# Mixer of a hybrid SSD/GLA layer: the router's product with its columns as the weights, in four column groups, added up one step later

## The chip, the cores and the metric

One core of one Trainium2 chip runs the whole program (one layer: modulation, input projection, two scans, mixer, mixture of experts, final norm). The metric is the device time of one execution in microseconds; lower is better. Below, T, L, P, N stand for names of the kernel; times are written in us.

## The reference, cut to what matters

The change lies in the stage that computes the token mixers' output, the residual, the second norm and the router's logits, for 2048 tokens in 16 tiles of 128 (D_MODEL = 1024, 32 experts):

```
mix = concat([y, o], -1) @ w_out
x = x + m_lat[2] * mix
h2 = modulate(rmsnorm(x, norm2_g), m_lat[3], m_lat[4])
s = jax.nn.sigmoid((h2 @ w_router).astype(jnp.float32))     # 2048 x 32
```

The product `h2 @ w_router` is what the change computes in another way. The scale of the modulation is applied to the tokens before it, and its shift enters as one row that is added to the logits (`rt_shift`).

## The kernel before, in words

`mixer` is written by hand, engine by engine; each engine runs its own list in the order of the code, and the engines meet only in semaphores. Its main loop has 18 steps n = 0 to 17 over 16 tiles (LT = 16). In a step three tiles are in work: `now` = n, `before` = n - 1 and `done` = n - 2 (`tiles(n)`).

TensorE's order in a step: `attn(now)` (L1626, eight products into `at`), `ssd(now)` (L1603 and L1611, into `py`), `turned_m(before)` (L1562, eight transposes into `tr`), `gla(now)` (L1644 and L1649, into `po`), `turned_x(done)` (L1570, eight transposes into `at`), `project(before)` (L1581, 48 products of 512 columns into `tr`) and `router(done)` (L1592). The router's product takes eight slices of 128 features: the turned tokens `xsT` (128x128) are the weights, the router's 32 columns `w_rt` the moving data, and the 128x32 result builds up in `po[:, 0, 256:288]`. Each f32 product stands in the trace as two passes.

VectorE's order: `masked_attn(now)` (L1768 twice, L1773), `state_mid` and `state_next` (L1688 to L1704), `split_m(before)` (L1755), `gated_y` (L1780, L1784), `segment` (L1732, L1738), `gated_o` (L1805, L1808), `decayed_scores` and `decayed_c` (L1746, L1751), then `residual(before)` (L1790), `scaled_x(before)` (L1798) and `logits(done)` (L1760). ScalarE ends a step with `squares_x(before)` (L1505), whose sum GpSimd turns into a reciprocal root (L1438, L1441) for `scaled_x`. `gla(now)` waits for both `both_done` (L1773) and `mid_done` (L1688) of the same step:

```
            def gla(t):
                r, qd = rec[t % 2], qks[t % 2][:, 0, :, :]
                pe.wait_ge(both_done, t + 1)
                pe.wait_ge(mid_done, t + CT + 1)
```

Elsewhere in the program two products already stand in the form with column groups: `slab_products` (L264) and the small columns of the input projection (L664), each `pe.matmul(acc[32 * j:32 * j + 32, ...], ...)` with j = k % 4.

The stage ends with a barrier of all engines (L1296 is the line of the semaphores' and the block's end); the next stage, `slots`, reads the logits.

Of the kernel before, what the change touches and what calls it, by code (L numbers as in the profile page):

```python
# [17 lines left out]
ALU = mybir.AluOpType  # L18
ACT = mybir.ActivationFunctionType
F32 = mybir.dt.float32  # L20
I32 = mybir.dt.int32
AX = mybir.AxisListType.X

P = 128
D = 1024
KT = D // P
# [6 lines left out]
LT = SEQ // P  # L33
SH, SP_, SN = 8, 64, 64
SW = SH * SP_
# [14 lines left out]
NE, NG, EG = 32, 8, 4  # L50
# [1239 lines left out]
def mixer(nc, A, C, K, route, tok_rec, feat_rec, back_state, fwd_chunk, qk_rec, a_rows, zg_rec, w_gated, x_mid, h_rows):  # L1290
    mod, ident = C["mod"], C["ident"]
# [4 lines left out]
    with ExitStack() as ctx:  # L1296
        sem = Names(nc, ctx, "mix")

        def sb(name, shape, dt=F32):
            return ctx.enter_context(nc.sbuf_tensor(f"{name}_m", shape, dt))  # L1300

        def ps(name):
            return ctx.enter_context(nc.psum_tensor(f"{name}_m", [P, 2, 512], F32))

        rec = [K["rec"][b][:, T_X:T_GF] for b in (2, 1)]
# [3 lines left out]
        st = [sb(f"st{b}", [P, 3, 256]) for b in range(2)]  # L1309
        abc = sb("abc", [P, 2, SH, P])  # L1310
        cs = sb("cs", [P, 2, 4, P])
        w_hi, w_lo = sb("w_hi", [P, KT, D], F32R), sb("w_lo", [P, KT, D], F32R)
        w_rt, rt_shift = sb("w_rt", [P, KT, NE]), sb("rt_shift", [P, NE])
        scale_bc, skip = sb("scale_bc", [P, D]), sb("skip", [P, SH])
        E, other = sb("E", [P, SH, P]), sb("other", [P, 4, P])
        M = sb("M", [P, SH, P])
# [5 lines left out]
        xs, xsT = sb("xs", [P, D]), sb("xsT", [P, KT, P])  # L1322
        ssm, ssx = sb("ssm", [P, 8]), sb("ssx", [P, 1])
        rs, rsx = sb("rs", [P, 8]), sb("rsx", [P, 1])
        py, po, at, tr = ps("py"), ps("po"), ps("at"), ps("tr")
# [18 lines left out]
        mt_ps, hi_done, lo_done, op_ps = (sem(n) for n in ("m_transposed", "m_hi_done", "m_lo_done", "out_product"))  # L1344
        x_added, x_sq, x_rs, xs_done, rows_added = (
            sem(n) for n in ("x_added", "x_square", "x_rstd", "x_scaled", "rows_added"))
        xt_ps, xt_done, log_ps, log_done = (sem(n) for n in ("x_transposed", "xT_done", "logits_product", "logits_done"))
        block = ctx.enter_context(nc.Block())

        def tiles(n):  # L1350
# [114 lines left out]
        @block.scalar  # L1465
        def _(act):
            def split_m(t, n):
                act.wait_ge(mt_ps, 2 * t + n + 1)
                act.activation(m_hi[:, 4 * n:4 * n + 4, :], tr[:, n, :].rearrange("p (a b) -> p a b", a=4), ACT.Copy).then_inc(hi_done, 1)

            def decays(t, g):
                act.wait_ge(seg_done, 2 * t + g + 1)
                act.activation(E[:, 4 * g:4 * g + 4, :], E[:, 4 * g:4 * g + 4, :], ACT.Exp).then_inc(seg_exp, 1)

            def inter_decays(t):
                act.wait_ge(cs_loaded, 64 * t + 64)
                act.activation(cs[:, :, :, :], cs[:, :, :, :], ACT.Exp).then_inc(cs_exp, 1)

            def turned_x(t):
                if t:  # L1480
                    act.wait_ge(log_ps, t)
                for n in range(2):
                    act.wait_ge(xt_ps, 2 * t + n + 1)
                    act.activation(xsT[:, 4 * n:4 * n + 4, :], at[:, n, :].rearrange("p (a b) -> p a b", a=4), ACT.Copy).then_inc(xt_done, 1)

            def squares_y(t):
                act.wait_ge(y_gated, t + 1)
                if t:
                    act.wait_ge(y_rs, t)
                    act.wait_ge(o_sq, 4 * t)  # L1490
                if t >= 2:
                    act.wait_ge(x_sq, t - 1)
                act.activation(junk[:, 0:SW], m[:, 0:SW], ACT.Square, scale=SW ** -0.5, accum_out=ssm[:, 4:5]).then_inc(y_sq, 1)

            def normed_y(t):
                act.wait_ge(y_rs, t + 1)
                act.activation(m[:, 0:SW], m[:, 0:SW], ACT.Copy, scale=rs[:, 4:5]).then_inc(y_done, 1)

            def squares_x(t):
                act.wait_ge(x_added, 2 * t + 2)  # L1500
                if t:
                    act.wait_ge(x_rs, t)
                act.wait_ge(y_sq, min(t + 2, LT))
                act.wait_ge(o_sq, 4 * min(t + 2, LT))
                act.activation(junk[:, :], x1[t % 2][:, :], ACT.Square, scale=D ** -0.5, accum_out=ssx[:, :]).then_inc(x_sq, 1)  # L1505

            def squares_o(t):
                act.wait_ge(o_ps, t + 1)
                if t:
                    act.wait_ge(o_rs, t)  # L1510
                act.wait_ge(y_sq, t + 1)
                for h in range(GH):
                    act.activation(junk[:, GV * h:GV * (h + 1)], po[:, h % 2, P * (h // 2):P * (h // 2 + 1)], ACT.Square, scale=GV ** -0.5,
                                   accum_out=ssm[:, h:h + 1]).then_inc(o_sq, 1)

            decays(0, 0)
            decays(0, 1)
            inter_decays(0)
            for n in range(LT + 2):
                now, before, done = tiles(n)  # L1520
                if before is not None:
                    split_m(before, 0)
                    split_m(before, 1)
                if now is not None:
                    squares_y(now)
                    squares_o(now)
                    normed_y(now)
                if done is not None:
                    turned_x(done)
                if now is not None:  # L1530
                    if now + 1 < LT:
                        decays(now + 1, 0)
                        decays(now + 1, 1)
                        inter_decays(now + 1)
                if before is not None:
                    squares_x(before)
                    act.dma_start(x_mid_t[before], x1[before % 2][:, :]).then_inc(x1_stored[before % 2], 16)

        @block.tensor
        def _(pe):  # L1540
# [45 lines left out]
            def router(t):  # L1586
                pe.wait_ge(xt_done, 2 * t + 2)
                pe.wait_ge(o_normed, min(t + 3, LT))
                if t:
                    pe.wait_ge(log_done, t)  # L1590
                for k in range(KT):
                    mm = pe.matmul(po[:, 0, 256:256 + NE], xsT[:, k, :], w_rt[:, k, :], start=(k == 0), stop=(k == KT - 1))  # L1592
                mm.then_inc(log_ps, 1)

            def ssd(t):
                h_f, h_b = st[t % 2], bst[t % 2]
# [58 lines left out]
            for n in range(LT + 2):  # L1655
                now, before, done = tiles(n)
                if now is not None:
                    attn(now)
                    ssd(now)
                if before is not None:  # L1660
                    turned_m(before, 0)
                    turned_m(before, 1)
                if now is not None:
                    gla(now)
                if n == 0:
                    router_shift()
                if done is not None:
                    turned_x(done)
                if before is not None:
                    project(before, range(KT))  # L1670
                if done is not None:
                    router(done)

        @block.vector
        def _(dve):
# [16 lines left out]
            def state_next(i, t):  # L1692
# [10 lines left out]
                dve.wait_ge(decayed, i + 1)  # L1703
                dve.tensor_tensor(nxt[:, 0, :], nxt[:, 0, :], f[:, 0:256], ALU.add).then_inc(next_done, 1)  # L1704

            for n, spread in enumerate((scale_bc, shift_bc)):
                dve.wait_ge(spread_ps, n + 1)
                for h in range(2):
                    dve.tensor_copy(spread[:, 512 * h:512 * h + 512], tr[:, h, :]).then_inc(spread_done, 1)
# [47 lines left out]

            def logits(t):
                dve.wait_ge(log_ps, t + 1)
                dve.tensor_tensor(route["logits"][:, t, :], po[:, 0, 256:256 + NE], rt_shift[:, :], ALU.add).then_inc(log_done, 1)  # L1760

            def masked_attn(t):
                if t:
# [50 lines left out]
            for n in range(LT + 2):  # L1814
                now, before, done = tiles(n)
                more = now is not None and now + 1 < LT
                if now is not None:
                    masked_attn(now)
                    state_mid(now + CT, now)
                    state_next(now + CT, now)  # L1820
                if before is not None:
                    split_m(before, 0)
                    split_m(before, 1)
                if now is not None:
                    gated_y(now)
                if more:
                    segment(now + 1, 0)
                    segment(now + 1, 1)
                if now is not None:
                    gated_o(now)  # L1830
                if n == 0:
                    router_shift()
                if more:
                    decayed_scores(now + 1)
                    decayed_c(now + 1)
                if before is not None:
                    residual(before)
                    scaled_x(before)
                if done is not None:
                    logits(done)  # L1840


TAB = MAXB + 4
# [635 lines left out]
```

## Time and profile before

| | us |
|---|---|
| median of 3 runs | 2337.08 (2336.34 to 2339.93) |
| the profiled execution's own time | 2337.34 |
| its span in the trace | 2335.5 |
| TensorE busy over the span | 2134.6 (91%) |
| VectorE busy | 1663.0 (71%) |
| ScalarE busy | 1159.2 (50%) |
| the mixer stage, from its first to its last work | about 855.6 to 1262 |

A row of the trace gives start, duration, engine, line and operation, output <- inputs; PE is TensorE's product, PEld its weight load, DVE VectorE, ACT ScalarE, POOL GpSimd. A duration of a product runs to the modelled arrival of its result, so rows of one engine overlap; how fast products follow on each other is read from starts.

### The profile page before, as it was taken

What the parts mean: (1) busy time and instruction counts of PE and PEld (TensorE: products, weight loads), DVE (VectorE), ACT (ScalarE), POOL (GpSimd) and SP (SyncE); (2) the same over time, 40 slices, a digit from 0 to 9 for tenths busy, and PEclk for the clock granted to TensorE, in tenths of its full rate; (3) what the DMA queues carried; (4) which work ended last, traced back from release to release, by engine and by line L of the source; (5) the groups of instructions that cost most, each with busy time, mean ns of one, the idle gap of its engine ahead of it and who ended that gap; (6) DMA issues with size and microseconds to landing.
All of it is one profiled execution on the core that took longest, in us unless ns stands there. A gap on an engine that the chain in (4) does not pass through costs nothing. (4 is left out here: it accounts for less than half of the span.)

```text
span 2335.5 us, 36752 instructions
## 1 busy us (share of the span) xinstructions
PE 2134.6 (91%) x11905; PEld 1734.7 (74%) x11905; DVE 1663.0 (71%) x2123; ACT 1159.2 (50%) x1499; POOL 513.7 (22%) x535
## 2 busy tenths in 40 slices
PE   5999999998999979999994499999999999999980
PEld 3888888886778768888883478778787878878760
DVE  2444444445776777677764789999999999999983
ACT  1233333334555533333331177777777777777763
POOL 1000000000010122233221123333332333343332
PEclk8999999998999997999996699999999999999995
DMA  8233333333888859898865345578978689899957
GB/s 329 68 120 120 120 120 120 120 111 104 307 300 301 309 176 362 290 309 289 306 186 165 142 141 174 162 235 277 334 237 289 209 258 369 265 328 312 373 167 300
DMA packets 209166, 537.27 MB, mean 230 GB/s; under 512 B 14896, under 2 KB 45611, under 8 KB 202539
## 3 DMA queue, kind: packets, MB, share of 16 engines
q1 hardware_dynamic: 176056, 424.71, 50.7%
q0 software_dynamic: 30512, 102.77, 16.9%
q10 hardware_dynamic: 2499, 8.45, 0.9%
q8 instruction: 63, 1.03, 0.2%
q14 instruction: 36, 0.29, 0.0%
HBM read 402.28 MB, written 133.61 MB: 229 GB/s over the span
## 5 line engine op out<-in xcount | busy, mean ns | idle before, releaser
L2217 ACT ACTIVATE w_hi_e<-w_gates 128x2048 fp32r (+1 forms) x103 | 197.9, 1923 | 212.1 <-issue 103.4
L2343 DVE TENSOR_TENSOR w_lo_e<-w_gates,w_hi_e 128x2048 fp32r<-128x2048 f32 x103 | 236.2, 2294 | 34.1 <-ACT w_hi_e L2217 34.1
L2343 DVE TENSOR_TENSOR w_lo_e<-w_ups,w_hi_e 128x2048 fp32r<-128x2048 f32 x102 | 233.3, 2288 | 36.9 <-ACT w_hi_e L2217 36.9
L2343 DVE TENSOR_TENSOR w_lo_e<-w_downs,w_hi_e 128x2048 fp32r<-128x2048 f32 x100 | 228.4, 2284 | 0.0
L2217 ACT ACTIVATE w_hi_e<-w_ups 128x2048 fp32r (+1 forms) x102 | 195.7, 1918 | 24.9 <-PE pd_e L2290 22.5
L2217 ACT ACTIVATE w_hi_e<-w_downs 128x2048 fp32r x100 | 191.6, 1916 | 0.8
L650 PE MATMUL pf<-raws,w_in_sb 128*128 128x256 f32 x800 | 176.1, 382 | 1.1 <-DVE raws L726 1.1
L2290 PE MATMUL pg_e<-w_hi_e,x_hi_e 128*128 128x512 f32 x408 | 167.7, 411 | 7.3 <-DVE w_lo_e L2343 7.3
L650 PEld LDWEIGHTS pf<-raws,w_in_sb 128*128 128x128 f32 x800 | 152.8, 192 | 22.5 <-DVE raws L726 1.5
L2195 POOL DMA_INDIRECT x_mid<-yb_e,to_e x50 | 127.6, 2551 | 185.1 <-DVE yb_e L2387 183.1
L2290 PE MATMUL pd_e<-w_hi_e,h_hi_e 128*128 128x512 f32 x400 | 162.2, 405 | 0.0
L2290 PE MATMUL pg_e<-w_lo_e,x_hi_e 128*128 128x512 f32 x408 | 161.9, 397 | 0.0
L2290 PE MATMUL pg_e<-w_hi_e,x_lo_e 128*128 128x512 f32 x408 | 161.8, 397 | 0.0
L2290 PE MATMUL pd_e<-w_hi_e,h_lo_e 128*128 128x512 f32 x400 | 157.9, 395 | 0.0
L2290 PE MATMUL pu_e<-w_hi_e,x_hi_e 128*128 128x512 f32 x400 | 157.8, 395 | 0.0
L2290 PE MATMUL pu_e<-w_hi_e,x_lo_e 128*128 128x512 f32 x400 | 157.8, 395 | 0.0
L2290 PE MATMUL pu_e<-w_lo_e,x_hi_e 128*128 128x512 f32 x400 | 157.8, 395 | 0.0
L2290 PE MATMUL pd_e<-w_lo_e,h_hi_e 128*128 128x512 f32 x400 | 157.8, 395 | 0.0
L2174 POOL COPY idx_e<-toks 128x1 int32 (+1 forms) x54 | 50.5, 936 | 450.3 <-DMA x_mid<-yb_e,to_e 341.9
L650 PE MATMUL pf<-hT,w_in_sb 128*128 128x256 f32 x640 | 139.5, 379 | 0.0
L650 PEld LDWEIGHTS pf<-hT,w_in_sb 128*128 128x128 f32 x640 | 121.3, 190 | 16.5
L757 DVE TENSOR_SCALAR fm<-u_raw,cols 128x256 f32<-128x256 f32 x54 | 18.3, 408 | 146.8 <-ACT u_raw L536 146.8
(423 smaller groups left out, 4839.2 us busy)
## 6 DMA issues: line engine op xcount, KB each, us to landing
w_gates<-in_w_gate_dram SPq DMA_DIRECT2D x32, 2048.0 KB, 11.9
w_ups<-in_w_up_dram SPq DMA_DIRECT2D x32, 2048.0 KB
w_downs<-in_w_down_dram SPq DMA_DIRECT2D x32, 2048.0 KB
w_mod_half<-in_w_mod_dram SPq DMA_DIRECT2D x16, 1024.0 KB, 6.6
abc_m<-a_rows SPq DMA_DIRECT2D x16, 1024.0 KB, 4.9
recs<-tok_rec SPq DMA_DIRECT2D x15, 968.0 KB, 7.8
qk_rec<-qk SPq DMA_DIRECT2D x14, 1024.0 KB, 3.9
qk<-qk_rec SPq DMA_DIRECT2D x14, 1024.0 KB
```

The costliest lines, as they stand in the source:

```text
L650: mm = pe.matmul(pf[n % 2][:, f, :], w[:, k, c0:c0 + P], h[:, k, :], start=(k == 0), stop=(k == KT - 1))
L757: i = dve.tensor_scalar(a, b, wt, cols[:, R_CB + f:R_CB + f + 1], ALU.mult, ALU.add)
L2174: pool.tensor_copy(idx[u][:, :], toks[:, bass.ds(b, 1), 0]).then_inc(idx_ready, 1)
L2195: pool.indirect_dma_start(out=x_mid, out_offset=bass.IndirectOffsetOnAxis(ap=to[u][:, 0:1], axis=0), in_=yb[:, :], in_offset=None, compute ...
L2217: act.activation(w_hi[:, s % 3:s % 3 + 1, :], raw(part, half, place), ACT.Copy).then_inc(hi_done, 1)
L2290: mm = pe.matmul(acc[:, :], a[:, k, :], w[:, s % 3, c], start=start and n == 0, stop=stop and n == 2)
L2343: dve.tensor_tensor(w_lo[:, s % 3:s % 3 + 1, :], raw(part, half, place), w_hi[:, s % 3:s % 3 + 1, :].bitcast(F32), ALU.subtract).then_inc( ...
```

## The change

The router's columns become the weights: for slice k the 32 columns `w_rt[:, k, :]` are loaded into column group j = k % 4 of the array, and the tokens `xsT[:, k, :]` (128 columns) stream past. Slices 0 to 3 start, slices 4 to 7 add, so four partial sums of 32x128 build up on partitions 32j to 32j + 31 of `po[:, 0, 256:384]`. ScalarE copies them into `quarters` (a part of a buffer of the stage before), and a product of `quarters` with `sum4` (128x32: four identities, one under another) adds the four and turns the result back to 128x32. This small product stands in the next step between `attn` and `ssd`; the logits' addition on VectorE moves from the end of a step to behind `masked_attn` of the next.

```diff
+        sum4, quarters = K["st"][0][:, 0, 0:NE], K["rec"][0][:, D + SW:D + SW + P]
...
             def turned_x(t):
                 if t:
-                    act.wait_ge(log_ps, t)
+                    act.wait_ge(quarter_ps, t)
...
+            def quartered(t):
+                act.wait_ge(quarter_ps, t + 1)
+                if t:
+                    act.wait_ge(log_ps, t)
+                act.activation(quarters[:, :], po[:, 0, 256:256 + P], ACT.Copy).then_inc(quarter_done, 1)
...
                         inter_decays(now + 1)
+                if done is not None:
+                    quartered(done)
                 if before is not None:
                     squares_x(before)
...
                 for k in range(KT):
-                    mm = pe.matmul(po[:, 0, 256:256 + NE], xsT[:, k, :], w_rt[:, k, :], start=(k == 0), stop=(k == KT - 1))
-                mm.then_inc(log_ps, 1)
+                    j = k % 4
+                    mm = pe.matmul(po[32 * j:32 * j + 32, 0, 256:256 + P], w_rt[:, k, :], xsT[:, k, :], start=(k < 4), stop=(k >= 4))
+                mm.then_inc(quarter_ps, 1)
+
+            def logit_sums(t):
+                pe.wait_ge(quarter_done, t + 1)
+                pe.wait_ge(sum4_done, 1)
+                pe.matmul(po[:, 0, 256 + P:256 + P + NE], quarters[:, :], sum4[:, :], start=True, stop=True).then_inc(log_ps, 1)
...
                     attn(now)
+                if n >= 3:
+                    logit_sums(n - 3)
+                if now is not None:
                     ssd(now)
...
+            logit_sums(LT - 1)
...
+            dve.tensor_reduce(sum4[:, :], ident[:, :].rearrange("p (j c) -> p c j", j=4), AX, ALU.add).then_inc(sum4_done, 1)
...
                     masked_attn(now)
+                if n >= 3:
+                    logits(n - 3)
+                if now is not None:
                     state_mid(now + CT, now)
...
-                if done is not None:
-                    logits(done)
+            logits(LT - 1)
```

What this moves on the engines is shown at one step boundary. TensorE, from the end of `project` of one step to `turned_m` of the next; the names are output <- weights or moving data, and the line numbers differ between the two kernels. Before:

```order
L1581 MATMUL tr_m<-w_hi_m,m_lo_m 128x512 x2
L1592 MATMUL po_m<-w_rt_m,xsT_m 128x32 x8
L1626 MATMUL at_m<-qk 128x128 x8
L1603 MATMUL py_m<-recs,M_m 128x64 x8
L1611 MATMUL py_m<-st_m,cs_m 128x64 x8
```

Now (`st` and `recs` in the fourth row are `sum4` and `quarters`):

```order
L1592 MATMUL tr_m<-w_hi_m,m_lo_m 128x512 x2
L1604 MATMUL po_m<-xsT_m,w_rt_m 32x128 x8
L1643 MATMUL at_m<-qk 128x128 x8
L1610 MATMUL po_m<-st,recs 128x32
L1620 MATMUL py_m<-recs,M_m 128x64 x8
L1628 MATMUL py_m<-st_m,cs_m 128x64 x8
```

The eight products keep their place, with their operands exchanged, and one product has come in ahead of `ssd`. VectorE over the same boundary, before:

```order
L1790 TENSOR_TENSOR x_m<-tr_m,x_m 128x512 x2
L1798 SCALAR_TENSOR_TENSOR xs_m<-x_m,rsx_m,scale_bc_m 128x1024
L1760 TENSOR_TENSOR logits<-po_m,rt_shift_m 128x32
L1768 TENSOR_TENSOR am_m<-at_m,incl_bd 128x512 x2
L1773 TENSOR_TENSOR both_m<-am_m 128x512
```

Now:

```order
L1812 TENSOR_TENSOR x_m<-tr_m,x_m 128x512 x2
L1820 SCALAR_TENSOR_TENSOR xs_m<-x_m,rsx_m,scale_bc_m 128x1024
L1790 TENSOR_TENSOR am_m<-at_m,incl_bd 128x512 x2
L1795 TENSOR_TENSOR both_m<-am_m 128x512
L1782 TENSOR_TENSOR logits<-po_m,rt_shift_m 128x32
L1709 SCALAR_TENSOR_TENSOR st_m<-st_m,fc 128x128 x2
```

The logits' addition has moved past three instructions and stands ahead of `state_mid` still. ScalarE at the end of a step, now (`recs<-po_m` is the copy of the quarters; the row was not there before, the others were):

```order
L1480 ACTIVATE cs_m<-cs_m 128x1024
L1493 ACTIVATE recs<-po_m 128x128
L1514 ACTIVATE recs,ssx_m<-x_m 128x1024
L1548 DMA x_mid<-x_m 128x1024
```

The copy has come in between the exponentials and `squares_x`.

## Rows read from the trace of the kernel before

**Rows 1.** The page: busy time of each engine over the span.
```profile
PE 2134.6 (91%) x11905; PEld 1734.7 (74%) x11905; DVE 1663.0 (71%) x2123; ACT 1159.2 (50%) x1499; POOL 513.7 (22%) x535
```

**Rows 2.** Stretches: one step; PE, PEld, DVE, ACT, POOL busy, clock, DMA, GB/s.
```profile
1093.36:1115.63 22.27, 22.27 (x186) 19.15 (x185) 16.33 (x28) 7.79 (x20) 6.92 (x9) 1.00 0.91 302
```

**Rows 3.** Timeline, TensorE, steps 9 to 10: start, us, engine, line, operation.
```profile
1093.36 1.98 PEld L1592 LDWEIGHTS po_m<-w_rt_m,xsT_m 128*128 128x128 f32 x16
1093.59 1.87 PE L1592 MATMUL po_m<-w_rt_m,xsT_m 128*128 128x32 f32 x16
...
1095.38 1.16 PE L1626 MATMUL at_m<-qk 64*128 64x128 f32 x16
...
1100.34 0.86 PEld L1562 LDWEIGHTS tr_m<-ident,m_m 128*128 128x128 f32 x8
...
1101.24 0.52 PEld L1644 LDWEIGHTS po_m<-recs,both_m 128*128 128x128 f32 x4
...
1103.13 0.45 PE L1649 MATMUL po_m<-st_m,qk 64*64 64x128 f32 x8
...
1103.72 0.86 PEld L1570 LDWEIGHTS at_m<-ident,xs_m 128*128 128x128 f32 x8 [0.17 <-issue]
...
1104.55 0.30 PEld L1581 LDWEIGHTS tr_m<-w_hi_m,m_hi_m 128*128 128x128 f32 x2
```

**Rows 4.** The same timeline: VectorE, ScalarE and GpSimd; in brackets idle time and releaser.
```profile
1093.63 1.29 DVE L1790 TENSOR_TENSOR x_m<-tr_m,x_m 128x512 f32<-128x512 f32 x2 [2.33 <-PE tr_m L1581]
1094.95 1.06 ACT L1505 ACTIVATE recs<-x_m 128x1024 f32<-128x1024 f32 x1 [6.25 <-DVE x_m L1790]
...
1096.57 0.57 POOL L1441 TENSOR_TENSOR rsx_m<-rsx_m,mhalf_m 128x1 f32<-128x1 f32 x1
1097.27 1.28 DVE L1798 SCALAR_TENSOR_TENSOR xs_m<-x_m,rsx_m,scale_bc_m 128x1024 f32<-128x1024 f32 x1 [2.35 <-POOL rsx_m L1441]
...
1098.47 0.18 DVE L1760 TENSOR_TENSOR logits<-po_m,rt_shift_m 128x32 f32<-128x32 f32 x1
1098.57 1.28 DVE L1768 TENSOR_TENSOR am_m<-at_m,incl_bd 128x512 f32<-128x512 f32 x2
...
1100.57 0.61 DVE L1688 SCALAR_TENSOR_TENSOR st_m<-st_m,fc 128x128 f32<-128x128 f32 x2
```

**Rows 5.** Timeline of step 2, the step without a router's product ahead of it.
```profile
921.64 0.68 PE L1644 MATMUL po_m<-recs,both_m 128*128 128x128 f32 x4 [1.77 <-DVE both_m L1773]
...
926.45 0.72 PE L1581 MATMUL tr_m<-w_hi_m,m_hi_m 128*128 128x512 f32 x2
```

**Rows 6.** Stretches behind that wait, and the stage's start; columns as in rows 2.
```profile
922.50:925.70 3.20, 3.20 (x37) 2.32 (x30) 3.17 (x6) 0.41 (x1) 0.00 (x0) 0.50 1.04 207
926.00:945.00 19.00, 19.00 (x140) 16.51 (x139) 11.59 (x19) 6.09 (x17) 6.92 (x9) 1.00 0.84 312
855.60:864.20 8.60, 4.07 (x32) 3.69 (x32) 5.69 (x12) 1.24 (x1) 0.06 (x1) 1.00 0.90 281
```

**Rows 7.** Timeline of the input projection: column groups with 256 moving columns.
```profile
203.12 0.56 PEld L664 LDWEIGHTS psm<-raws,w_small 128*32 128x32 f32 x12 [0.30 <-issue]
203.12 1.05 PE L664 MATMUL psm<-raws,w_small 128*32 128x256 f32 x16
204.10 0.50 PE L630 MATMUL pz<-wv_hi,x_hi 128*128 128x512 f32 x1
```

**Rows 8.** Timeline, ScalarE: one square of 128x128 read from `po`.
```profile
1105.76 0.28 ACT L1513 ACTIVATE recs<-po_m 128x128 f32<-128x128 f32 x1
```

**Rows 9.** Timeline, VectorE, the stage's first work; a reduction of 128 elements.
```profile
857.73 1.29 DVE L1709 COPY scale_bc_m<-tr_m 128x512 f32<-128x512 f32 x2 [0.44 <-PE tr_m L1545]
1269.03 0.29 DVE L1983 TENSOR_REDUCE best_r<-gscore_r 128x16 f32<-128x128 f32 x1
```

**Rows 10.** The stage's end: timeline, and line L1296 (ns min/median/max, starts).
```profile
1253.81 3.62 PE L1592 MATMUL po_m<-w_rt_m,xsT_m 128*128 128x32 f32 x16 [0.69 <-ACT xsT_m L1484]
1257.46 0.19 DVE L1760 TENSOR_TENSOR logits<-po_m,rt_shift_m 128x32 f32<-128x32 f32 x1 [6.27 <-PE po_m L1592]
...
L1296 POOLq DRAIN  x1: 3972/3972/3972, 1257.3 to 1257.3; - x1
L1296 SPq EVENT_SEMAPHORE  x1: 17/17/17, 1261.4 to 1261.4; - x1
```

More of the change, by code:

```diff
@@ L1346, in mixer @@
             sem(n) for n in ("x_added", "x_square", "x_rstd", "x_scaled", "rows_added"))
-        xt_ps, xt_done, log_ps, log_done = (sem(n) for n in ("x_transposed", "xT_done", "logits_product", "logits_done"))
+        xt_ps, xt_done, quarter_ps, quarter_done, log_ps, log_done = (
+            sem(n) for n in ("x_transposed", "xT_done", "logit_quarters", "quarters_copied", "logits_product", "logits_done"))
+        sum4_done = sem("sum_4_done")
         block = ctx.enter_context(nc.Block())
@@ L1759, in logits @@
                 dve.wait_ge(log_ps, t + 1)
-                dve.tensor_tensor(route["logits"][:, t, :], po[:, 0, 256:256 + NE], rt_shift[:, :], ALU.add).then_inc(log_done, 1)
+                dve.tensor_tensor(route["logits"][:, t, :], po[:, 0, 256 + P:256 + P + NE], rt_shift[:, :], ALU.add).then_inc(log_done, 1)
             def masked_attn(t):
```

## The prediction, before the change was run

> **What bounds the kernel now.** I read the page first, then stretches of the mixer, then its timeline, engine by engine. The page makes TensorE the suspect: 91% of the span [rows 1]. The stretch of one whole step of the mixer's loop says it more strongly: TensorE is busy for 22.27 of 22.27 us at the full clock, VectorE for 16.33, ScalarE for 7.79 [rows 2]. By that view alone, whatever shortens a product shortens the step. The timeline shows what it hides. Call T the start of the router's first weight load, which stands right behind the last projection product: 1093.36 [rows 3]. From T two chains run side by side until `gla`.
>
> TensorE's: router (to 1095.38), `attn`, `ssd`, then eight transposes whose first load starts at 1100.34, then `gla`, whose first load starts at 1101.24, that is T + 7.88 [rows 3].
>
> The other: the last projection product lets VectorE add the residual (1093.63, 1.29), ScalarE square (1094.95), GpSimd take the root (1096.57), VectorE scale (1097.27), add the logits (1098.47), mask the attention scores (1098.57), add them and update the state; `state_mid` starts at 1100.57 and runs 0.61, so ends at 1101.18 = T + 7.82 [rows 4]. VectorE's 2.33 and 2.35 of idle time in this chain are latency, not slack.
>
> `gla` waits for both. Its load starts 0.06 after `state_mid` ends. Would it have started earlier without that wait? The same eight transposes stand a second time in a step, where nothing is waited for behind them: load 1103.72 to the next load 1104.55, 0.83 [rows 3]. From 1100.34 that gives 1101.17, where `gla` loads at 1101.24. So TensorE arrives 0.07 before the state is there: the two chains end together, and VectorE's is the later one by a hair. The 100% busy step is the sum of two halves, of which one (T to `gla`) is set by the chain over four engines.
>
> **The change, part by part**, as times after T.
>
> *Router's product.* Before: T to the first `attn` product, 2.02 (16 passes of a full 128x128 load, 1.79 / 16 = 0.11 each) [rows 3]. Now 16 passes, four at a time, of 128 moving columns. The trace has no such row; two are near. `gla`'s own 16 passes of 128 f32 columns on four tiles of 64x64, which start at 1103.13 with the transposes following at 1103.72: 0.59 with the change of tile size behind it [rows 3]. And the input projection's 16 passes on the very 128x32 tiles, but with 256 columns: 203.12 to 204.10, 0.98 [rows 7]. I take 0.59, since the columns agree, and keep 0.98 as the upper end. Ahead of it stand 0.23 in which the last projection product streams (1093.36 to 1093.59) and, an estimate from how much of the 0.59 is not passes, 0.1 for the change of tile size. So `attn` starts at about T + 0.92 (at most 1.31), 1.1 earlier (at least 0.7).
>
> Here the Trainium skill speaks against the change: TensorE: Matmul & The Clock Gate, Part 3, says that weight loads overlap running products only when their row groups differ, and four column groups share all rows. By that rule the loads would line up with the products (the second rival prices this). The trace disagrees: twelve loads of L664 lie in 0.56 from 203.12 on, inside the products' time [rows 7].
>
> *The small product.* Two passes with a full load and 32 columns, 2 x 0.11 = 0.22, on TensorE between `attn` and `ssd`. It waits for ScalarE's copy, see next; TensorE gets there at about T + 2.1, so it doesn't wait.
>
> *ScalarE's copy.* The last pass's result is there at about T + 1.0 (at most 1.4). The copy reads 128x128 from `po`, as the squares of `gla`'s result do in 0.28 [rows 8]; with 0.05 for the semaphore it ends at T + 1.33 (at most 1.73). Queued behind it is `squares_x`, a link of the chain that sets the step; it needs ScalarE at 1094.95 = T + 1.59 [rows 4]. So the copy fits by 0.26; at the upper end it is late by 0.14, in each of 15 steps (n = 2 to 16): +2.1. I take 0. ScalarE is idle for 6.25 before that point [rows 4], which covers it.
>
> *The logits' addition.* It leaves the place ahead of `masked_attn`, where it costs 0.10 (1098.47 to 1098.57) [rows 4], and returns behind it, still ahead of `state_mid`. `both` comes 0.10 earlier, `state_mid` does not: T + 7.82 as before. I take 0; if the short addition were hidden at its new place, 13 x 0.10 = -1.3 would follow.
>
> *What comes of it on TensorE.* It reaches `gla` 1.1 - 0.22 = 0.88 earlier, T + 6.9, and waits there for the state until T + 7.88. From `gla`'s load to the end of `project` nothing is changed (3.31 to 1104.55, then 48 products). **Steps 3 to 15 (13 of them) gain 0.** In step 16 there is no `gla`; `turned_x` waits for `scaled_x`, which is the same chain: 0. `ssd` ends earlier, so the DMAs that wait for it are issued some 0.9 earlier for data wanted most of a step later: 0.
>
> *The start.* The reduction that makes `sum4` is new on VectorE, about 0.29 (a reduction of 128 elements), and stands where VectorE waits 0.44 for TensorE [rows 9]: 0. Without that cover it would cost 0.3 once.
>
> *The end.* In step 17 the last router's product runs at the reduced clock, 3.62, and the last logits end at 1257.65 [rows 10]. With groups, copy and small product this ends about 1 us earlier. But the stage ends for GpSimd: its queue drains for 3.97 from 1257.3 (behind the last store's landing), and all engines go on at 1261.4 [rows 10]. The cover is 3.6 us, so: 0.
>
> **The sum** is 0 against the profiled execution's 2337.34, which lies 0.26 above the median of the runs, 2337.08. Forecast 2337.0.
>
> **The rivals.**
>
> *1. TensorE is the bound after all* (busy all 22.27 [rows 2]). Then each of 13 steps gives 0.88: -11.4, about 2326. Against it: `gla`'s load starts 0.06 to 0.07 after `state_mid`'s end in each of these steps alike, and step 2, which has no router's product ahead of it, shows the outcome already: TensorE waits 1.77 ahead of `gla` for VectorE [rows 5]. Chance 0.04.
>
> *2. The copy comes late and holds up `squares_x`.* It decides from the point where the copy ends after T + 1.59, so where the product's result comes after T + 1.26. If the passes kept their old 0.11: 0.33 + 1.79 + 0.28 = T + 2.4, the copy ends at 2.73, 1.14 late, 15 times: +17, about 2354. Against it: the two rows of four tiles. Over 0.2% needs 0.31 per step, twice what my upper end leaves. Chance 0.02. If on top of that loads and products took turns, 0.11 and 0.11 per pass, it would be 16 x 0.11 = 1.8 more in each step, 15 x 2.9 = +44, about 2381: chance 0.01, since the loads there do overlap [rows 7]. (That is what the Trainium skill's rule on row groups, named above, would come to here.)
>
> *3. The clock.* The wait that takes the place of the work is about 0.95 in each of 13 steps. In step 2, behind TensorE's wait of 1.77, the granted clock stood at 0.50 from 922.5 to 925.7, and at 1.00 again from 926 [rows 5, 6]; from `gla` to `project` it took 926.45 - 921.64 = 4.81, where a step at full clock takes 3.31: a price of 1.5. Every step hit: 13 x 1.5 = +19.5, about 2356.5; it goes past 0.2% (4.7) with four steps of 13. For it: the section from T to `gla` is already thin work. Against it: the wait is about half as long, and at the stage's start TensorE was busy for 4.07 of 8.60 us with the clock at 1.00 throughout [rows 6]. Chance 0.06 for four steps or more, and about 0.1 for one to three (+1.5 to +4.5).
>
> **How the numbers follow.** A measurement of this kernel tells about 0.2%, 4.7 us, from no change. My own case, no change of the path, has 0.87 with the small clock cases in it; its time is 2337.0. The range reaches down by the 1.3 of the hidden addition and 1 for the spread of runs, to 2334.7, and up by the 2.1 of the copy, or two steps hit by the clock (3.0), and the same 1: 2341.0. Faster by over 0.2%: rival 1 and what I have not thought of, 0.05. Slower by over 0.2%: rivals 2 and 3, 0.09. Within: 0.86.
>
> **What would show it.** Right: the new product's rows from its first product to `attn` near 0.6; the copy ending before 1.59 after T; a new idle time of TensorE ahead of `gla`, about 0.9, put down to VectorE, in 13 steps; steps of 22.27 as before; the clock at 1.00 from 926 to the last steps. TensorE's busy time falls by some 10 us while the span stays. Wrong: steps shorter than 22.2 (the chain was not the bound); `squares_x` later than 1.59 after T (rival 2); stretches at 0.50 between 930 and 1230, and steps of about 23.8 (rival 3).

## The result, and the profile after

| | before | after |
|---|---|---|
| median of 16 runs each, same chip | 2338.32 (2333.64 to 2343.31) | 2342.12 (2337.90 to 2347.41) |
| ratio, 95% interval | | 1.0016 (1.0009 to 1.0022) |
| profiled execution, its span | 2337.34, 2335.5 | 2342.06, 2340.3 |

The median lies 1.1 us above the upper end of the range, 2341.0. The ratio stays under the 0.2% that was called a difference, but its interval excludes 1: the change costs a little, where the forecast was nothing. By the ratio alone the change costs 2.1 to 5.1 us. Of the 5.1 us between the forecast of 2337.0 and the median, 1.3 are not the change's: the forecast took the median of three runs, 2337.08, and the same kernel's median over 16 runs, those three among them, is 2338.32. It was 2338.53 to 2338.84 in the three later comparisons with many runs too.

The page's busy line of the changed kernel, to [rows 1], and one row of its costliest groups (engine, tile, count; busy and mean ns; idle time ahead of it, most of it without a releaser, "issue"):

```profile
PE 2120.3 (91%) x11937; PEld 1712.7 (73%) x11937; DVE 1663.1 (71%) x2124; ACT 1163.0 (50%) x1515; POOL 509.9 (22%) x535
...
L2241 ACT ACTIVATE w_hi_e<-w_gates 128x2048 fp32r (+1 forms) x103 | 197.9, 1923 | 213.8 <-issue 107.8
```

TensorE is busy for 14.3 us less (2134.6 before) and the span is no shorter. One step of the loop, columns as in [rows 2], a stretch of the whole loop, and the stretch behind the wait in step 2, which answers to the first of [rows 6]:

```profile
1094.94:1117.21 22.27, 21.52 (x188) 17.80 (x186) 16.33 (x28) 8.06 (x21) 6.92 (x9) 1.00 0.91 313
...
930.00:1230.00 300.00, 289.85 (x2476) 239.26 (x2474) 211.12 (x362) 104.51 (x274) 88.55 (x118) 1.00 0.83 274
...
921.50:928.00 6.50, 6.17 (x49) 5.09 (x50) 6.43 (x14) 2.02 (x11) 1.46 (x3) 0.50 1.06 299
```

The timeline of that step answers to [rows 3, 4]. T is 1094.94 here, counted back from the residual's addition, which starts 0.27 behind T in both kernels:

```profile
1095.21 1.29 DVE L1812 TENSOR_TENSOR x_m<-tr_m,x_m 128x512 f32<-128x512 f32 x2 [2.35 <-PE tr_m L1592]
1095.26 0.64 PE L1604 MATMUL po_m<-xsT_m,w_rt_m 128*32 128x128 f32 x16
1095.84 1.16 PE L1643 MATMUL at_m<-qk 64*128 64x128 f32 x16
1095.97 0.28 ACT L1493 ACTIVATE recs<-po_m 128x128 f32<-128x128 f32 x1 [5.71 <-PE po_m L1604]
1096.54 1.06 ACT L1514 ACTIVATE recs<-x_m 128x1024 f32<-128x1024 f32 x1 [0.28 <-DVE x_m L1812]
1096.93 0.41 PE L1610 MATMUL po_m<-st,recs 128*128 128x32 f32 x2
...
1102.15 0.60 DVE L1709 SCALAR_TENSOR_TENSOR st_m<-st_m,fc 128x128 f32<-128x128 f32 x2
1102.83 0.52 PEld L1661 LDWEIGHTS po_m<-recs,both_m 128*128 128x128 f32 x4 [0.96 <-DVE both_m L1795]
1102.86 0.68 PE L1661 MATMUL po_m<-recs,both_m 128*128 128x128 f32 x4 [0.75 <-DVE st_m L1709]
```

The reader is to see three things. The sixteen passes take 0.58 (1095.26 to 1095.84). The copy (L1493) is over at 1096.25, 0.29 before `squares_x` (L1514). And `gla` now has a wait ahead of it, 0.96 on its weight load, put down to VectorE. The load starts at 1102.83, 0.08 after `state_mid` ends (1102.15 + 0.60 = 1102.75). `gla` starts at T + 7.89, where it started before at T + 7.88: the work taken from TensorE became that wait.

**Where the profiled execution's +4.8 of span lies**, from marks that both timelines have (starts of the same products in each):

| stretch | before | after | |
|---|---|---|---|
| start of the program to T of step 1 | 913.50 | 913.45 | -0.05 |
| T of step 1 to T of step 2 | 24.00 | 25.62 | +1.62 |
| step 3 | 22.26 | 22.26 | 0 |
| steps 4 to 15 | 267.20 | 267.21 | +0.01 |
| step 16 | 18.94 | 19.18 | +0.24 |
| from there to the first work of `slots` | 16.40 | 18.19 | +1.79 |
| to the sixth block of the experts' loop | 160.84 | 160.74 | -0.10 |
| experts' loop from there to its last product, 23 rounds | 842.04 | 843.03 | +0.99 |
| the rest | 70.34 | 70.61 | +0.27 |

The mixer's thirteen steps hold none of it. Three places hold nearly all of it, and the forecast named none of them as a cost. The first is step 2, which has no router's product ahead of it: after its wait the granted clock stood at 0.50 (1.2 GHz, the lower of its two levels; 1.00 is 2.4 GHz) for 3.4 us before [rows 6] and for 6.8 us now. The second is the stage's end: the last store of `h_rows` landed 7.4 after its issue where it took 5.7 before, and GpSimd's drain, 3.97 as in [rows 10], began at 1260.9 instead of 1257.3:

```profile
L1296 POOLq DRAIN  x1: 3972/3972/3972, 1260.9 to 1260.9; - x1
```

The third is the experts' loop, whose code the change does not touch. The runs had to say which of these the change causes and which differ from one execution to the next anyway.

### The profile page after: what moved, and what is told of

Same layout as the page of the kernel before. It is cut to its first block and busy times, and to the rows that moved or that the text cites. A ratio compares the mean times of both kernels' runs of the same rounds, so it can differ in the third digit from the quotient of the medians.

```text
span 2340.3 us, 36863 instructions
## 1 busy us (share of the span) xinstructions
PE 2120.3 (91%) x11937; PEld 1712.7 (73%) x11937; DVE 1663.1 (71%) x2124; ACT 1163.0 (50%) x1515; POOL 509.9 (22%) x535
## 3 DMA queue, kind: packets, MB, share of 16 engines
q8 instruction: 63, 1.03, 0.2%
## 5 line engine op out<-in xcount | busy, mean ns | idle before, releaser
L2241 ACT ACTIVATE w_hi_e<-w_gates 128x2048 fp32r (+1 forms) x103 | 197.9, 1923 | 213.8 <-issue 107.8
## 6 DMA issues: line engine op xcount, KB each, us to landing
w_ups<-in_w_up_dram SPq DMA_DIRECT2D x32, 2048.0 KB, 16.3
```

The source lines that it names most:

```text
L2241: act.activation(w_hi[:, s % 3:s % 3 + 1, :], raw(part, half, place), ACT.Copy).then_inc(hi_done, 1)
```

## The experiments

Theory A: the wait that replaced TensorE's work costs clock (rival 3 in another dress). Theory B: the first result is scatter of executions. Theory C: the last store of the mixer lands later with the change, and the stage's end with it. Theory D: the changed kernel gives ScalarE 31 instructions more (16 copies, 15 semaphore waits) ahead of the experts' loop, and where the loop lies in its program sets the time of the loop's edge.

**Both kernels again.** The kernel before, unchanged.

> The kernel before, a second time, for a second profile of it and for the noise of the comparison. All theories: ratio 1.000 with an interval of about 0.1%. Theory A (the clock): behind TensorE's wait in step 2 and in step 16 the granted clock falls to 0.50 here as well, for a time that differs from execution to execution, 3 to 7 us; the 13 steps in between are 22.27 each. Theory C (the last store): the last store of the mixer lands 5.7 us after its issue, as in the first profile of this kernel (7.5 in that of the changed one); theory B (scatter) says that it differs between executions of one kernel, so it may be 7 here.

Measured: 2336.89, ratio 0.9994 (0.9985 to 1.0003). The same program against itself came out 0.6 thousandths off, so less than about 1.5 us is nothing that a single comparison shows.

> The changed kernel, a second time. Theory A: slower than before by about 4 us (1.0016), with more time at clock 0.50 than the kernel before has, in step 16 above all, where TensorE now idles about 1 us longer. Theory B: the 3.8 us are mostly scatter; ratio within 1.0000 to 1.0010, and its rows differ from the first profile's by as much as from the kernel before. Theory C: slower by about 2 us or more, with the last store landing more than 7 us after its issue and the stage's end 1.8 us later. All: 13 steps of 22.27 and a wait of TensorE of about 0.95 ahead of gla in each.

Measured: 2340.50, ratio 1.0008 (0.9998 to 1.0017): half of the first ratio. Step 2 and the stage's end in the new traces:

```profile
914.00:945.00 31.00, 28.59 (x268) 24.85 (x264) 22.77 (x42) 10.14 (x24) 9.24 (x13) 1.00 0.93 324
```

That is the kernel before: no stretch at 0.50 behind the wait at all, and T to T took 23.13. The changed kernel took 26.27 in this execution, with 6.8 at 0.50. At the stage's end the repeat of the changed kernel took 16.08 where its first profile took 18.19 (16.40 and 16.47 in the two of the kernel before). So the first two of the three places differ between executions of one kernel. The late store is the less settled of the two: in the seven profiles with the router's old form it landed 5.3 to 5.7 after its issue, in those with the new form 7.4 once, 6.0 once and 5.3 to 5.6 five times. Other places differ as well. T of step 1 lies between 912.15 and 917.27 in the fourteen profiles (913.45 and 915.61 in the two of the changed kernel), and step 16 takes 18.84 to 19.84 in the six with the old router and VectorE's old order, so its +0.24 shows nothing. The experts' loop doesn't differ: it took 842.00 and 843.04, as in the first pair.

**Filled wait.** Four of the products in their old form, into a part of `at` that the next work overwrites, keep TensorE at work where it would wait. What is stored is unchanged.

```diff
 def router(t):
...
+                for k in range(4):
+                    pe.matmul(at[:, 0, 0:NE], xsT[:, k, :], w_rt[:, k, :], start=(k == 0), stop=(k == 3))
```

> The changed kernel with four products in the old form (tokens as weights, 32 columns) put behind each router product into a free part of the attention scores' PSUM; their result is thrown away. They give TensorE back about 0.9 us of the 1.1 us of work per step that the change took away, so it no longer waits ahead of gla and idles in step 16 as before. Theory A: back to the kernel before, ratio 1.000 (under 1.0007), TensorE busy 22.2 of 22.27 in a step. Theory B or C, and anything that sits in ScalarE's copies or in the tail: no change against the changed kernel, 1.0010 to 1.0020.

Measured: 2339.69, ratio 1.0014 (1.0005 to 1.0023); the quotient of the two medians alone would be 1.0005. TensorE is busy for 298.43 of 300 us (299.96 in the kernel before), and by the ratio the time is not back. Its profiled execution was the fastest of its eleven, 2335.10, with the clock at 1.00 in step 16 too, where the thirteen other profiles, those of the kernel before among them, have 3.4 or 6.8 us at 0.50. So theory A has no support in the thirteen steps: in none of the profiles of the changed kernel does the clock leave 1.00 in steps 3 to 15. Here is the stretch with the products added:

```profile
930.00:1230.00 300.00, 298.43 (x2582) 250.53 (x2580) 211.70 (x363) 106.24 (x277) 88.75 (x119) 1.00 0.83 275
```

**Instructions alone.** The kernel before, with 31 instructions more on ScalarE at the end of its mixer list, all waits on a semaphore that is long past 1 (two of them go into one instruction). The trace counts 32, the 31 and a branch that comes with them; 16, 48 and 64 below are 17, 49 and 65 in the same way. No copy, no groups, no small product.

```diff
+            for _ in range(63):
+                act.wait_ge(x_sq, 1)
```

> The kernel before, with 31 instructions added to ScalarE's program (waits on a semaphore that has long passed) at the end of its list in the mixer, where ScalarE idles for microseconds: as many as the change adds to it. TensorE's, VectorE's work and the router stay as before. Theory D (placement): the experts' loop, 25 rounds of two blocks each, takes 0.04 us longer in each round whenever ScalarE's program ahead of it is 31 instructions longer: w_hi_e<-w_gates starts 0.07 us later at the loop's edge; the loop ends 1.0 us later (from its 40th product to its last 843.0 in place of 842.0), with nothing of the change in the kernel; ratio about 1.0004 to 1.0008. Theory A (clock and idle time) or any theory that looks in the mixer: 842.0, ratio 1.000.

Measured: 2339.20, ratio 1.0004 (0.9995 to 1.0014), which by itself decides nothing. Its trace does. The same line of ScalarE, once in each round of the experts' loop and twenty rounds apart, before, after, and in this kernel:

```profile
1417.90 1.92 ACT L2217 ACTIVATE w_hi_e<-w_gates 128x2048 fp32r x1 [0.89 <-PE pd_e L2290]
...
1532.98 1.93 ACT L2217 ACTIVATE w_hi_e<-w_gates 128x2048 fp32r x1 [2.49 <-issue]
...
2155.59 1.92 ACT L2217 ACTIVATE w_hi_e<-w_gates 128x2048 fp32r x1 [0.89 <-PE pd_e L2290]
```

```profile
1421.43 1.92 ACT L2241 ACTIVATE w_hi_e<-w_gates 128x2048 fp32r x1 [0.89 <-PE pd_e L2314]
...
1536.70 1.92 ACT L2241 ACTIVATE w_hi_e<-w_gates 128x2048 fp32r x1 [2.55 <-issue]
...
2160.00 1.92 ACT L2241 ACTIVATE w_hi_e<-w_gates 128x2048 fp32r x1 [0.89 <-PE pd_e L2314]
```

```profile
1418.03 1.92 ACT L2219 ACTIVATE w_hi_e<-w_gates 128x2048 fp32r x1 [0.89 <-PE pd_e L2292]
...
1533.29 1.92 ACT L2219 ACTIVATE w_hi_e<-w_gates 128x2048 fp32r x1 [2.55 <-issue]
...
2156.47 1.93 ACT L2219 ACTIVATE w_hi_e<-w_gates 128x2048 fp32r x1 [0.89 <-PE pd_e L2292]
```

Twenty rounds took 737.69, 738.57 and 738.44. The middle row of each fence is the first weight conversion behind the loop's edge. ScalarE waits for nothing there that the profile shows, and comes to it 0.06 later in the two longer programs. TensorE waits for this weight through VectorE's `w_lo_e`, and its idle time ahead of `pg_e` at that point is 0.47 before and 0.51 or 0.52 in both others. So these instructions alone give the loop's +1. The page's row of that line says it shortest: idle time without a releaser is 103.4 before, 107.8 after and 107.7 here.

**One instruction more.** The changed kernel with one instruction added in the same way (with its branch 33 in all by the trace, where the change alone has 31).

```diff
+            for _ in range(3):
+                act.wait_ge(x_sq, 1)
```

> The changed kernel with one more such instruction on ScalarE, 32 more than before in all. Theory D: if the loop's edge depends on where the code lies, one instruction can take the 0.07 us away again (842.0), or it stays (843.0); either way the mixer's 13 steps stay at 22.27. A theory that the 0.04 us come from what the mixer leaves behind (addresses, semaphores, time): 843.0.

Measured: 2340.18, ratio 1.0009 (1.0000 to 1.0018), loop 842.95. Two places further change nothing.

**Other lengths.** The kernel before with 16, 48 and 64 instructions (`range(33)`, `range(97)`, `range(129)`), each profiled once.

> The kernel before with 16 added instructions on ScalarE in place of 31, at the same place. Theory D: if what counts is where the experts' loop lies in ScalarE's program, the cost at the loop's edge can be there or not (issue time ahead of w_hi_e<-w_gates 107.8 or 103.4, the loop 843.0 or 842.0 from its 40th product on); if it grows with the number of instructions, it is half: 105.6 and 842.5.

> The same with 48. By growth with the number: issue 110 and 843.5. By place: one of the two values, 103.4 and 842.0 or 107.8 and 843.0.

> The same with 64. By growth: issue 112.5 and 844. By place with a period that divides 64 instructions: as without any, 103.4 and 842.0.

Measured, as the loop from its sixth block to its last product: 842.02 with 16, 842.95 with 48 and 838.70 with 64. The issue time is 103.4, 107.7 and 103.4. The values are steady. With no instruction more, or 16, all four profiles give 841.96 to 842.04; with 31, 32 or 48 all eight (the changed kernel and its variants among them) give 842.93 to 843.07; with 64 it is 838.70. The edge with 64 instructions in the timeline, TensorE in one round and ScalarE in the next:

```profile
1502.82 0.19 PEld L2292 LDWEIGHTS pg_e<-w_hi_e,x_hi_e 128*128 128x128 f32 x1 [0.33 <-DVE w_lo_e L2345]
...
1535.12 1.92 ACT L2219 ACTIVATE w_hi_e<-w_gates 128x2048 fp32r x1 [2.36 <-issue]
```

The conversion comes 0.13 earlier than before, TensorE waits 0.33 instead of 0.47. The rows of ScalarE's sequencer, in which a round has 122 instructions, show where these times arise. Between one instruction and the next stands a delay of 0.07 in all eight profiles with 31 to 49 added (by the trace's count), and it moves with the added instructions: counted from the branch that closes the round, it stands ahead of the 30th instruction with 31 added, of the 29th with 32, of the 28th with 33 and of the 12th with 49. So it belongs to one fixed place in ScalarE's program. With none or 17 that place is the 61st or 44th, behind the 34th, a semaphore wait that takes up such differences, and no delay is seen. With 65 it lies ahead of the loop; and there the instruction behind the closing branch starts 0.14 after it, where it is 0.27 in the twelve other profiles. These are the +0.06 and the -0.13 of the conversion. What ends at that place, and why the branch is then cheaper, isn't shown.

One candidate falls: that ScalarE's instructions are loaded anew by DMA in each round. The queues that load instructions moved one to three packets between 1360 and 2260, in 24 rounds, in every one of the fourteen profiles. The Trainium skill (Advanced Engine Details and Errata, ISA Cache) gives a cache of two lines of 16 KB, 256 instructions each. By that, a loop of 122 instructions lies across two lines at most and needs no loading anew. The trace agrees, also with the size (the page's queue row has 63 packets with 1.03 MB, 16.3 KB each).

**Is the freed time of TensorE worth anything?** Where the router's product saves 0.9 per step and VectorE's chain takes it back, a shorter chain should give it back. First the small step: `state_mid` of the next tile moves from behind `masked_attn` to between the residual and `scaled_x`, where VectorE waits for GpSimd's root ([rows 4], 2.35 idle).

```diff
+            state_mid(CT, 0)
...
-                    state_mid(now + CT, now)
...
                     residual(before)
+                if more:
+                    state_mid(now + 1 + CT, now + 1)
                 if before is not None:
                     scaled_x(before)
```

> The changed kernel with state_mid of the next step issued on VectorE between residual and scaled_x, in the 2.35 us that VectorE waits there for GpSimd, in place of behind the logits. If the chain over VectorE sets T to gla, as I predicted, gla starts 0.5 earlier after T (7.3 to 7.4 in place of 7.88, as both_done and then the semaphore set it), the step becomes 21.7 to 21.8, and the kernel is 13 x 0.5 = 6.5 to 7 us faster than the changed one: ratio to before 0.9985 to 0.999 (by theory A with up to 3 us of clock on top of it). If the chain was not the bound, the step stays 22.27.

Measured: 2332.86, ratio 0.9977 (0.9968 to 0.9986), lower than the 0.9985 expected. The steps take 21.78 to 21.81 instead of 22.27, as expected, and TensorE's wait ahead of `gla` is halved and stands on `both_m` alone:

```profile
1092.28 0.61 DVE L1709 SCALAR_TENSOR_TENSOR st_m<-st_m,fc 128x128 f32<-128x128 f32 x2
...
1097.31 0.69 DVE L1795 TENSOR_TENSOR both_m<-am_m 128x512 f32<-128x512 f32 x1
1098.22 0.52 PEld L1661 LDWEIGHTS po_m<-recs,both_m 128*128 128x128 f32 x4 [0.48 <-DVE both_m L1795]
```

Then both: `masked_attn` and `state_mid` of the next tile move there, once in the changed kernel and once in the kernel before.

```diff
+            masked_attn(0)
+            state_mid(CT, 0)
...
-                if now is not None:
-                    masked_attn(now)
...
-                    state_mid(now + CT, now)
...
+                if more:
+                    masked_attn(now + 1)
+                    state_mid(now + 1 + CT, now + 1)
                 if before is not None:
                     scaled_x(before)
```

> The changed kernel with masked_attn and state_mid of the next step between residual and scaled_x on VectorE. The attention product is there at about T + 2.05 with the change, so the 1.9 us of masking fit into VectorE's 2.35 us of idle time and gla waits for neither. If my reading holds, TensorE becomes the bound and all of the 0.94 us shows: gla at T + 6.9 to 7.0, steps of 21.3 to 21.4, 12 us in 13 steps: ratio to before 0.995 to 0.9965. If instead the time of T to gla were set by something that both kernels share (PSUM, semaphores), the steps stay near 21.8 as in the run with state_mid alone.

> The kernel before (router in its old form) with the same move on VectorE. TensorE is then the bound at its old amount of work: it reached gla 0.07 us before the state was there, so steps of 22.19 to 22.21, about 1 us in 13 steps; ratio 0.9995 to 1.000. The difference between this kernel and the last one is then what the router's new product is worth where TensorE is the bound: 0.85 to 0.9 us a step. A rival, that VectorE's order alone brings the gain: steps of 21.3 to 21.8 here too.

Measured: the changed kernel with the move 2324.63, ratio 0.9938 (0.9925 to 0.9952); the kernel before with it 2334.21, ratio 0.9980 (0.9971 to 0.9989). Both ratios are lower than expected, where only the thirteen steps were counted (step 2 below is the rest). A step of the first, its `gla`, and the `gla` of the second:

```profile
1082.57:1103.86 21.29, 21.29 (x188) 17.78 (x186) 16.41 (x28) 8.09 (x21) 6.91 (x9) 1.00 0.90 313
```

```profile
1083.46 1.16 PE L1643 MATMUL at_m<-qk 64*128 64x128 f32 x16
1084.74 1.29 DVE L1790 TENSOR_TENSOR am_m<-at_m,incl_bd 128x512 f32<-128x512 f32 x2 [0.62 <-PE at_m L1643]
1086.13 0.69 DVE L1795 TENSOR_TENSOR both_m<-am_m 128x512 f32<-128x512 f32 x1
1086.74 0.61 DVE L1709 SCALAR_TENSOR_TENSOR st_m<-st_m,fc 128x128 f32<-128x128 f32 x2
...
1089.46 0.53 PEld L1661 LDWEIGHTS po_m<-recs,both_m 128*128 128x128 f32 x4
```

```profile
1090.08 1.98 PEld L1592 LDWEIGHTS po_m<-w_rt_m,xsT_m 128*128 128x128 f32 x16
1092.10 1.16 PE L1626 MATMUL at_m<-qk 64*128 64x128 f32 x16
...
1097.88 0.53 PEld L1644 LDWEIGHTS po_m<-recs,both_m 128*128 128x128 f32 x4
```

Neither `gla` has a wait ahead of it now; both steps are TensorE's own. From T the first loads at 6.89 (T = 1082.57), the second at 7.80, and steps take 21.29 and 22.18 to 22.21. The difference, 0.9 per step and 11.7 over 13 steps, is what the router's change saves where TensorE sets the pace. The two medians lie only 9.6 apart: the loop and the stretch behind it, 1.1 and 0.6 longer with the change, are most of the difference. In the kernel before the move gave 0.07 per step, as the seven hundredths by which VectorE's chain was the later one would have it. The rest of that kernel's gain is step 2, where VectorE was late by more: 24.00 there became 20.5 in both.

**Both findings together.** The moved work, and 33 waits on ScalarE, which with the change's own 31 make 64:

```diff
+            for _ in range(67):
+                act.wait_ge(x_sq, 1)
```

> The changed kernel with VectorE's order of the earlier run (masked_attn and state_mid ahead of scaled_x) and 33 added instructions on ScalarE, so that its program ahead of the experts' loop is 64 instructions longer than in the kernel before, as in the run with 64 on the old kernel. Theory D: the experts' loop takes 838.7 from its 40th product on, as there, in place of 843.0, and the steps of the mixer 21.29: about 4.8 us under the run without the added instructions (2324.6), 2320, ratio about 0.992. A rival, that the 838.7 were a chance of one execution: 843.0 and no gain over 0.9938.

Measured: 2318.40, ratio 0.9915 (0.9903 to 0.9928), the fastest of all. The loop took 838.63, as with 64 before; that is 4.4 of the 6.2 between this median and 2324.63, and 0.4 more lies behind the loop. The other 1.4 isn't located, and the two ran on different chips. The page has 208.8 of idle time ahead of this line, where it has 213.8 in the changed kernel and 209.6 in the kernel before with 64:

```profile
L2246 ACT ACTIVATE w_hi_e<-w_gates 128x2048 fp32r (+1 forms) x103 | 198.0, 1923 | 208.8 <-issue 103.4
```

## Why the prediction was right in the mixer and wrong in the sum

- *Router's product, 0.59 taken, 0.98 at most:* 0.58. The row of `gla`'s own passes with as many columns was the right one, and the passes overlap across the four groups; a price of 0.11 for each would have been 1.79. `attn` came at T + 0.90 (T + 0.92 forecast). The Trainium skill's rule on row groups (TensorE: Matmul & The Clock Gate, Part 3), weighed in the prediction, is contradicted once more: in the changed kernel's step the 16 loads lie in 0.38 from 1095.26 on, inside the products' 0.58.
- *Small product:* it starts at 1096.93 = T + 1.99 without a wait, as forecast.
- *Copy:* over at T + 1.31 (T + 1.33), `squares_x` at T + 1.60 as before. Rival 2 is out.
- *Logits, start:* no difference in a step; `sum4`'s reduction took 0.38, and the copies behind it began at 856.77, where [rows 9] has 857.73.
- *TensorE and `gla`:* a wait of 0.95 to 0.96 (0.95 forecast), on VectorE, in all 13 steps, and a step of 22.27. Rival 1 is out, by the loop and by the two kernels with VectorE's work moved: the bound was where [rows 3, 4] had it.
- *Clock:* the 13 new waits never cost clock. Rival 3 is out. One argument against it was weaker than it looked: the stretch at the stage's start in [rows 6] ends at 864.2, and from 864.4 on the clock stood at 0.50 for 37.5 us in that same trace. Step 2's price, 1.5 in the prediction, turned out to differ by execution: 0, 3.4 or 6.8 us at 0.50 behind it. T to T there was 22.01 to 26.19 in six profiles with the old router, and 22.09 to 26.27 in five with the new one (the three with `masked_attn` moved left aside). It belongs to neither kernel.
- *End:* the last router's product and its logits take 2.15 (1255.63 to 1257.78) instead of 3.65 (1253.81 to 1257.46), more than the 1 forecast, and hidden behind GpSimd's drain as forecast. The 1.8 by which that drain began late, relative to the steps, did not come back in the repeat.

The base was low as well: the three runs that the forecast had gave 1.2 less than the 16 did, which is more than the 1.1 by which the median passed the range.

**The step that failed is the sum: "The sum is 0".** It counted the mixer's steps, start and end, and took every stage behind it as the same. The 31 instructions that the change adds to ScalarE were costed where they run, in idle time, at 0, which is right, and not for what they push back. The experts' loop, 1.0 us longer in each of the six profiles of the changed kernel and its variants, and in the kernel before with 31 or 48 instructions more, is the measured term. Behind the loop, from its last product to the end of the span, it was 70.34 to 70.48 in the five profiles with the old router and none, 16 or 64 instructions more, 70.94 and 70.89 with 31 and 48, and 70.61 to 71.17 (mean 70.92) in the six with the change: 0.5 more. Together about 1.5 us, which no term of the forecast and no part of its range stood for.

That does not make up the first comparison's 3.8. It makes up most of the repeat's 2.0 (2340.50 against 2338.53), and lies in the interval of the kernel that has the instructions alone, which also holds no change at all. Of the two largest pieces of the first profiled execution, step 2's 1.6 goes both ways in both kernels; the last store's 1.8 did not come back in the repeat, but was not seen with the old router either. Whether the change shifts how often they occur isn't shown. So some 1.5 us are accounted for, all of it found too where the instructions were added alone; a remainder of some 0.5 (repeat) to 2.3 us (first comparison) stays open.

The prediction's list of what would prove it right (product near 0.6, copy before T + 1.59, wait near 0.9 on VectorE, steps of 22.27, clock at 1.00 from 926) came out in each line but the last, whose date moved to 928.2 with step 2's stretch at 0.50, and the one for the span.

## What to carry to other kernels

An engine that is busy for the whole of a step may still not be its bound: compare, at the point where two chains meet, when the one's last product of work ends and when the other arrives, to the hundredth. Whoever shortens one of two equally long chains gains nothing until the other one is shortened too; here each alone gave 0 and 0.07 per step, and both together 0.98. And count the instructions that a change puts ahead of a hot loop on each engine: compare the idle time put down to "issue" at the loop's edge in both profiles, before a difference of a few tenths of a per cent is put down to the change itself.

## What the runs showed that I had not expected

- The length of ScalarE's program ahead of the loop changed the loop's speed, in both directions: per round of 36.9 us +0.04 with 31 to 48 instructions more (eight profiles), -0.145 with 64 (two). With 64 GpSimd's indirect DMA to `x_mid` also shows 3.53 us a piece where it showed 2.57, while GpSimd's program is unchanged; why isn't known.
- Behind one and the same wait in step 2 (1.3 to 2.9 us of idle TensorE) the clock fell to 0.50 for 0, 3.4 or 6.8 us in different executions. In ten of the eleven profiles the longer wait had the longer time (0 behind 1.29 to 1.43, 3.4 behind 1.77 twice, 6.8 behind 2.01 to 2.89); the eleventh had 0 behind 2.42. Thirteen waits of 0.96, one per 22.27, never made it fall.
- Four column groups of 32 with f32 and 128 moving columns cost 0.58 for 16 passes, 0.036 each, a third of the 0.11 of a pass with the whole array in the router's old form.
